# Block 2's first FFN behind its norm: low parts of the first two weight units in whole quarters, five of them held until the third token chunk, and PE's tiles in another order

## The reference

```python
h = h + rms_norm(ffn, norm_gains[layer, 3])          # end of block 1
...
def swiglu(x, w_in, w_out):
    gate, up = jnp.split(x @ w_in, 2, axis=-1)
    return (jax.nn.silu(gate) * up) @ w_out
...
h = h + 0.5 * swiglu(rms_norm_2(h, ffn1_norm[i]), ffn1_w_in[i], ffn1_w_out[i])   # start of block 2
```

## Time and profile before

| | |
|---|---|
| median of 3 runs | 2176.37 us (2175.43 to 2178.03) |
| profiled execution, its own time | 2177.4 us |
| its span | 2175.6 us |
| PE busy | 2143.6 us (99%) |
| DVE, ACT, POOL busy | 994.2, 756.6, 1010.3 us |
| POOL, low parts of the weights (L709) | 1009.0 us in 820 instructions |

### The profile page before, as it was taken

How to read it: one execution, slowest core, us unless ns; L and a number is a source line. 1 busy time by engine, 2 the same in 40 slices (tenths; PEclk the granted TensorE clock), 3 DMA queues, 4 the chain that set the end, 5 groups by cost and what they waited for, 6 DMA issues and landing times.

```text
span 2175.6 us, 31348 instructions
## 1 busy us (share of the span) xinstructions
PE 2143.6 (99%) x12490; PEld 1848.4 (85%) x12490; DVE 994.2 (46%) x1459; ACT 756.6 (35%) x1018; POOL 1010.3 (46%) x825
## 2 busy tenths in 40 slices
PE   8999999999999999999999999999999999999998
PEld 7897999999999887888888788878788888888886
DVE  5144454379888207322200829671876442222027
ACT  4133455243222216322212415551336332222134
POOL 4322223455555547555544545254331555555444
PEclk9999999999999999999999999999999999999999
DMA  4321111212222223322222221114220222222222
GB/s 165 103 69 69 59 44 74 97 59 97 96 92 83 108 95 111 120 96 96 97 97 96 102 101 44 57 60 153 78 78 21 97 97 97 96 96 97 96 101 93
DMA packets 31950, 195.17 MB, mean 90 GB/s; under 512 B 3968, under 2 KB 4480, under 8 KB 10096
## 3 DMA queue, kind: packets, MB, share of 16 engines
q1 hardware_dynamic: 26352, 182.66, 23.4%
q10 hardware_dynamic: 5504, 11.18, 1.6%
HBM read 189.47 MB, written 4.23 MB: 89 GB/s over the span
## 4 chain that ended last, share of the span: by engine, by line
PE 82%; issue 7%; DVE 5%; POOL 4%; ACT 1%; DMA 0%; SPq 0%; DVEq 0%; POOLq 0%; ACTq 0%
PE ps L2377 72%; POOL wlo L709 4%; PE ps L2972 2%; DVE sqa L1527 1%; PE ps L3187 1%; PE ps L3171 1%; PE ps L3054 1%; DVE x2lo L1515 1%; PE ps L3107 1%; PE ps L2656 1%; PE ps L2679 0%; PE ps L3152 0%; PE ps L2715 0%; PE ps L3197 0%; DMA h<-h 0%
## 5 line engine op out<-in xcount | busy, mean ns | idle before, releaser
L709 POOL TENSOR_TENSOR wlo<-raw,whi 128x512 fp32r<-128x512 f32 (+2 forms) x820 | 1009.0, 1263 | 1139.4 <-ACT whi L775 1035.4
L775 ACT CAST whi<-raw 128x2048 fp32r<-128x2048 f32 x162 | 309.6, 1911 | 810.7 <-PE ps L2377 753.3
L2377 PE MATMUL ps<-x2hi,whi 128*128 128x512 f32 x1136 | 448.9, 395 | 1.2 <-DVE x2lo L1515 1.1
L2377 PE MATMUL ps<-x2hi,wlo 128*128 128x512 f32 x1136 | 442.6, 390 | 0.0
L2377 PE MATMUL ps<-x2lo,whi 128*128 128x512 f32 x1136 | 442.4, 389 | 0.0
L2377 PE MATMUL ps<-xhi,whi 128*128 128x256 f32 (+2 forms) x1336 | 271.5, 285 | 12.2 <-DVE xlo L1581 9.3
L2377 PE MATMUL ps<-xlo,whi 128*128 128x256 f32 (+2 forms) x1336 | 270.0, 284 | 0.0
L2377 PE MATMUL ps<-xhi,wlo 128*128 128x256 f32 (+2 forms) x1336 | 269.9, 283 | 0.0
L2377 PEld LDWEIGHTS ps<-x2hi,whi 128*128 128x128 f32 x1136 | 213.4, 188 | 49.6 <-issue 4.8
L2377 PEld LDWEIGHTS ps<-x2lo,whi 128*128 128x128 f32 x1136 | 213.5, 188 | 44.6 <-issue 1.7
L2377 PEld LDWEIGHTS ps<-x2hi,wlo 128*128 128x128 f32 x1136 | 213.3, 188 | 44.3
(11 more groups left out here) (472 smaller groups left out, 2759.9 us busy)
## 6 DMA issues: line engine op xcount, KB each, us to landing
raw<-wstream SPq DMA_DIRECT2D x170, 1024.0 KB, 4.8
h<-h SPq DMA_DIRECT2D x4, 528.0 KB, 8.7
ncb<-c_rows ACTq DMA_DIRECT2D x8, 256.0 KB, 3.5
ple_rows<-ple_out ACTq DMA_DIRECT2D x4, 512.0 KB, 4.0
bias<-bias_rows ACTq DMA_DIRECT2D x8, 256.0 KB, 4.6
ple<-ple_rows ACTq DMA_DIRECT2D x4, 512.0 KB, 5.5
out_dram<-outb SPq DMA_DIRECT2D x8, 256.0 KB, 2.9
raw<-wstream ACTq DMA_DIRECT2D x4, 256.0 KB, 7.3
```

Source lines behind the costliest of these rows:

```text
L709: return nc.gpsimd.tensor_tensor(wlo[b][:, cols], raw[b][:, cols], whi[b][:, cols].bitcast(F32), ALU.subtract)
L775: nc.scalar.copy(whi[b][:], raw[b][:]).then_inc(sig("hi_done"), 1)
L2377: ins = mm(dst, w[slot][:, cols], xx(tok), start=first and p_ == 0, stop=last and p_ == 2, skip_group_check=True)
```

## The change

The two units leave the list of those with pieces of 128 columns, so that each of their quarters is one instruction of 128x512. Their eight quarters get an order of their own on POOL, three first and five later, and between the two groups POOL waits until the third token chunk is ready. `lo_first` is counted by that order (`LO_ORDER`), and PE's `low_ready` looks its place up there. PE's list has the first two entries of the value unit ahead of the gate unit's third, and others shifted.

```diff
-        PIECE = {u: P for u in (U_UP, U_UP + 1, U_PLEP, U_F1I, U_F1I + 1, U_GR + 2, U_GR + 3, U_MG1, U_DSAO + 1)}
+        PIECE = {u: P for u in (U_UP, U_UP + 1, U_PLEP, U_GR + 2, U_GR + 3, U_MG1, U_DSAO + 1)}
         QUARTERED = [0, U_UP + 1, U_UP + 2, U_PLEP, U_F1I, U_F1I + 1, U_F1I + 2, U_PLEG + 3]
-        PIECE[U_F1I + 2] = PIECE[U_UP + 2] = BANK
+        PIECE[U_F1I] = PIECE[U_F1I + 1] = PIECE[U_F1I + 2] = PIECE[U_UP + 2] = BANK
+        LO_ORDER = [(u, q) for u in QUARTERED for q in range(3)]
+        FIRST_LOW = [(U_F1I, 0), (U_F1I, 1), (U_F1I + 1, 0)]
+        LATER_LOW = [(U_F1I + 1, 1), (U_F1I, 2), (U_F1I, 3), (U_F1I + 1, 2), (U_F1I + 1, 3)]
+        at_f1 = LO_ORDER.index((U_F1I, 0))
+        LO_ORDER[at_f1:at_f1 + 6] = [(u, q) for u, q in FIRST_LOW + LATER_LOW if q < 3]
...
+            def low_of_two(order):
+
+                for u, q in order:
+                    if u == U_F1I:
+                        pool.wait_ge(sig("hi_done"), u + 1)
+                    elif q < 3:
+                        pool.wait_ge(sig("hi_first"), 3 * HI_FIRST.index(u) + q + 1)
+                    else:
+                        pool.wait_ge(sig("hi_done"), u + 1)
+                    low_part(u % 2, q).then_inc(sig("lo_first" if q < 3 else "lo_done"), 1)
...
-                    low_parts(u, PIECE.get(u, BANK))
+                    if u == U_F1I:
+                        low_of_two(FIRST_LOW)
+                        pool.wait_ge(sig("x_ready"), RAW[4] + 3)
+                        low_of_two(LATER_LOW)
+                    elif u != U_F1I + 1:
+                        low_parts(u, PIECE.get(u, BANK))
...
-                    pe.wait_ge(sig("lo_first"), 3 * QUARTERED.index(u) + q + 1)
+                    pe.wait_ge(sig("lo_first"), LO_ORDER.index((u, q)) + 1)
...
-            after_ple = [(0, 0), (0, 1), (0, 2), (1, 0), (1, 1), (0, 3), (0, 4), (1, 2), (0, 5), (1, 3), (0, 6), (0, 7)]
...
+            after_ple = [(0, 0), (0, 1), (1, 0), (1, 1), (0, 2), (0, 3), (1, 2), (0, 4), (1, 3), (0, 5), (1, 4), (0, 6)]
+            after_ple += [(0, 7), (1, 5), (1, 6), (1, 7)]
```

More of the change, by code:

```diff
@@ L2927, in swiglu @@
                 down(unit0 + FC, layer)
-            after_ple = [(0, 0), (0, 1), (0, 2), (1, 0), (1, 1), (0, 3), (0, 4), (1, 2), (0, 5), (1, 3), (0, 6), (0, 7)]
-            after_ple += [(1, k) for k in range(4, KC)]
+            after_ple = [(0, 0), (0, 1), (1, 0), (1, 1), (0, 2), (0, 3), (1, 2), (0, 4), (1, 3), (0, 5), (1, 4), (0, 6)]
+            after_ple += [(0, 7), (1, 5), (1, 6), (1, 7)]
             swiglu(U_F1I, 1, after_ple)
```

## The result

The changed kernel took 2179.56 us (median of 20 runs, 2176.37 to 2180.99), the kernel before 2176.47 (20 runs); the ratio is 1.0013, with a 95% interval of 1.0007 to 1.0019. So it is slower, by 3.1 us, and within the 0.2% that the prediction called no change. The time lies in the range, 1.9 us above the number forecast.

What follows compares the result with a forecast made beforehand. PE was taken to bound the kernel, with norm 4 also needing DVE's sums. PE (865.8) and DVE (866.0) late together gave +1.3 us: 2178.7 for an execution like the profiled 2177.4, median 2177.7, range 2174.6 to 2180.0.

Steps and rivals of the forecast that it cites:

- Sum: Norm 4 on PE starts at 866.1 us instead of 864.83, +1.3 us.
- R2: Rival: TensorE's clock falls in PE's pauses, 3.4 us lost, +4.7 us in all, 2181.1 us; chance 0.06.
- Per quarter it is the same: A POOL quarter costs DVE 1.1 us whole, 1.08 in four pieces; only the collisions' place can win.
- Step (5): Behind the held quarters DVE takes 2.08 us a chunk instead of 2.61; its last chunk is 2.4 us late.
- R1: Rival: a whole quarter stops DVE for less than four pieces do; -2.15 us, 2174.2 us; chance 0.15.
- Steps (1) and (4): POOL's first two quarters end at 833.5; five held ones each meet one DVE instruction, 1.70 us apart, lo(4) 3.8 late.
- Step (2): The second unit's first quarter meets one DVE instruction, costing 1.1 us; nt(3) ends about 842.5, 0.7 earlier than before.
- Step (3): DVE's gain before the third chunk is not cashed: it waits about 1.2 us for ACT's x2hi; chunk ready at 844.4.
- Step (6): DVE's seven norm sums take 0.80 us each alone; only the last meets a following unit's quarter; end at 866.0.
- Step (7): PE pauses 0.7 us ahead of the fourth chunk and 2.4 ahead of the fifth, ending at 865.8.
- Step (8): Behind norm 4, the next unit's low parts arrive in time; slack shrinks from some 3 to 1.4 us.
- R3: Rival: POOL's hold does not hold because the third chunk is already ready; +0.6 us, 2177.0 us; chance 0.11.

Runs made afterwards that it cites:

- v2: Change's low-part and PE orders, but 128-column pieces, no hold, norm 4 after the next unit's first four tiles; against the kernel before: 2175.91 us, 0.9996.

## Why the prediction was right, and where it was off

- *Sum +1.3, measured +1.7 or +2.9.* Two executions of four have the tail 1.72 and 1.80 longer, the other two 2.92 and 2.93. The forecast describes the former, 0.4 to 0.5 short. The latter show the sign by which it called itself wrong, the drop of the granted clock, at less than the +4.7 of its rival R2, to which it gave 0.06. That the median still lies in the range is in part luck: by its interval the change costs 1.5 to 4.1 us, more than the +1.3, and the range goes to 2180.0 because 1.0 us of spread between runs was put on top of its +2.6.
- *"Per quarter it is the same": wrong.* Beside this chain of instructions a held quarter costs DVE 0.96 us whole and about 0.53 in pieces (by the run that is held, but in pieces). The 0.27 a piece was read where the next DVE instruction could start 0.60 behind the last; one of the three of a chunk, x2lo, starts 0.87 behind in any case. Step (5) had this, with 2.08 us for a chunk without POOL and 2.61 with pieces: 0.53 for three pieces, not 0.81. The sum went by 1.70, 2.08 and 2.61 as read, so the error is not in it. But the change loses by the size of the collisions and not only by their place, and among the rivals only R1 had the sizes differ, the other way round.
- *Steps (1) and (4): right.* The pairing of one quarter with one DVE instruction, 1.70 apart, holds to the hundredth; five collisions, as counted. *Step (2): right in kind, 0.3 off:* one collision, but nt(3) ends at 842.90 (0.12 of it the shift of the whole trace against before) where 842.5 was worked out, since lo(1) waits for its x2hi too. *Step (5): right,* at 2.14 us for a chunk instead of 2.08 (h starts at 853.77 and 855.91).
- *Step (3): right in kind, 0.25 off.* The gain before the third chunk is not cashed; DVE waits 1.12 for x2hi (about 1.2 forecast). But ACT's chain is not closed: x2hi(1) waits for h(1), which came 0.25 later, so x2hi(2) starts at 843.26 instead of 842.91, 0.12 of that again the shift. This and the longer chunks of step (5) are the missing 0.4: the sums begin at 860.19 where 859.65 was worked out.
- *Step (6): the last sum meets C's first quarter,* as said, where the clock stays up (6.36 us for the seven sums there); where it falls C comes later and none does (5.46).
- *Step (7): right.* Pauses 0.84 and 2.10 to 2.14 against 0.7 and 2.4.
- *Step (8): right.* Nothing behind the norm waits in the changed kernel. In v2, where the norm moved, a wait on low parts did come, but on those of the unit behind C.
- *R2, the term mis-sized.* It put the loss at 3.4 us and let it count only where the clock is at half for more than 6 us. Measured are 3.4 us at half clock behind pauses of 0.84 and 2.10 us, PE later by 1.7, the time by 1.2, in half of the traces. The step that failed is its evidence against: that full work on both sides keeps the clock up. It does so only sometimes. The Trainium skill, page "TensorE: Matmul & The Clock Gate", Part 1, calls the slow start of a kernel run-variable: the same kernel measures different numbers of slow matmuls. It says so of the start and not of a pause; behind a pause the traces here show the like (two with the fall, two without, same pauses).
- *R1:* out; DVE's instructions beside quarters take 1.75 to 1.78. *R3:* out; POOL idles 6.57 us.
- *The parts, by the tails.* PE's new order with the new order of low parts, in pieces and without the hold: -0.13. Whole quarters instead of pieces: 1.4 more (+1.25). The hold: 0.5 more (about +1.75). The fall of the clock, where it comes: 1.2 more (+2.92).

## What to carry to other kernels

Ask what a collision costs the chain that it delays, not what it costs one instruction. Cutting POOL's work fine made it dearer for POOL (16.43 us instead of 8.44 for five quarters) and cheaper for DVE (0.53 a quarter instead of 0.96), because part of the small collisions fell where DVE waits for ACT anyway, and it spread them, so that PE, which eats DVE's output, did not run dry; whole quarters, even fewer and later, made PE pause. A pause of TensorE can cost more than its length: look at the granted clock behind it, in several traces. When one wait is taken away, look at once at what had been queued behind it: half of the gain expected of v2 was lost to a cast that nobody had waited for until then.

## What the runs showed that I had not expected

- A pause of 2.1 us, some 5 us behind one of 0.84, with full work around them, was followed by TensorE's clock at half (granted 0.51) for 3.4 us in two of four executions, 1.5 us behind the pause in one and 0.5 in the other. Behind the pause of 1.94 us in the trace of PE's order alone and that of 3.33 in PE's old order it fell too; behind that of 2.11 us in the kernel without the hold and those of 1.64 and 1.67 in two kernels with pieces it did not. In these traces the length of a pause alone does not tell.
- A POOL instruction does not block DVE for its whole length: where DVE's next instruction has all that it needs, a piece of 0.45 us costs it 0.27, a quarter of 1.29 us 1.1.
